# Recurrent mixer: the convolution's first tap moved from VectorE to ScalarE, the other three taps one unit later

## The reference, cut to what matters

```python
def causal_depthwise_conv(x, w, b):
    k_width = w.shape[0]
    s = x.shape[1]
    xp = jnp.pad(x, ((0, 0), (k_width - 1, 0), (0, 0)))
    out = b + xp[:, 0:s] * w[0]
    for k in range(1, k_width):
        out = out + xp[:, k:k + s] * w[k]
    return out

def recurrent_mixer(x, w_in, conv_w, conv_b, gate_a_w, gate_a_b, gate_x_w, gate_x_b, lam, w_out):
    y, r = jnp.split(x @ w_in, 2, axis=-1)
    y = jax.nn.gelu(y)
    r = causal_depthwise_conv(r, conv_w, conv_b)
    h = rg_lru(r, gate_a_w, gate_a_b, gate_x_w, gate_x_b, lam)
    return (y * h) @ w_out
```

## Time and profile before

| | before |
|---|---|
| median of 3 runs | 1528.91 us |
| lowest, highest | 1522.83, 1529.1 us |
| the profiled execution | 1525.94 us |
| its span | 1524.0 us |
| TensorE, VectorE, ScalarE, GpSimd busy | 97%, 69%, 50%, 21% of the span |
| mean granted TensorE clock | 0.994 of full speed |

### The profile page before, as it was taken

How to read it: one execution, slowest core, us unless ns; L and a number is a source line. 1 busy time by engine, 2 the same in 40 slices (tenths; PEclk the granted TensorE clock), 3 DMA queues, 4 the chain that set the end, 5 groups by cost and what they waited for, 6 DMA issues and landing times.

```text
span 1524.0 us, 31453 instructions
## 1 busy us (share of the span) xinstructions
PE 1480.7 (97%) x11939; PEld 1460.6 (96%) x11939; DVE 1052.0 (69%) x1999; ACT 765.5 (50%) x1270; POOL 318.6 (21%) x392
## 2 busy tenths in 40 slices
PE   7999998999999999999999999999999999999998
PEld 7999998899999999999999999889999999899898
DVE  6666578766655666557766656888678778876883
ACT  5454448555444554445554545446644453565442
POOL 4111113211101111014321114453320125231000
PEclk9999999999999999999999999999999999999999
DMA  6656754465555655554565555533343554334333
GB/s 207 186 179 200 241 166 139 152 189 184 181 174 185 186 184 181 173 188 154 162 192 180 179 176 157 152 107 116 91 119 107 164 145 123 99 98 125 111 117 120
DMA packets 245275, 239.65 MB, mean 157 GB/s; under 512 B 15160, under 2 KB 244392, under 8 KB 245048
## 3 DMA queue, kind: packets, MB, share of 16 engines
q1 hardware_dynamic: 245176, 238.29, 50.9%
HBM read 237.21 MB, written 1.05 MB: 156 GB/s over the span
## 4 chain that ended last, share of the span: by engine, by line
PE 84%; DVE 10%; ACT 2%; issue 2%; POOL 1%; DMA 0%; SPq 0%; DVEq 0%; ACTq 0%; POOLq 0%
PE bank L552 25%; PE bank L554 25%; PE bank L553 25%; DVE w_lo L1523 3%; PE bank L878 1%; PE bank L818 1%; PE bank L836 1%; ACT w_hi L967 1%; PE bank L801 1%; DVE work L1563 1%; DVE work L1680 1%; PE bank L884 1%; PE bank L894 1%; PE bank L817 1%; PE bank L837 0%
## 5 line engine op out<-in xcount | busy, mean ns | idle before, releaser
L1523 DVE TENSOR_TENSOR w_lo<-raw,w_hi 128x1024 fp32r<-128x1024 f32 (+1 forms) x456 | 563.0, 1244 | 303.8 <-ACT w_hi L967 303.5
L552 PE MATMUL bank<-x_hi,w_hi 128*128 128x256 f32 (+1 forms) x2480 | 719.0, 290 | 2.2 <-DVE w_lo L1523 2.2
L554 PE MATMUL bank<-x_hi,w_lo 128*128 128x256 f32 (+1 forms) x2480 | 707.1, 285 | 0.0
L553 PE MATMUL bank<-x_lo,w_hi 128*128 128x256 f32 (+1 forms) x2480 | 706.2, 285 | 0.0
L967 ACT CAST w_hi<-raw 128x1024 fp32r<-128x1024 f32 (+1 forms) x456 | 464.9, 1030 | 261.2 <-PE bank L554 250.1
L552 PEld LDWEIGHTS bank<-x_hi,w_hi 128*128 128x128 f32 x2480 | 476.0, 192 | 4.1 <-issue 2.0
L553 PEld LDWEIGHTS bank<-x_lo,w_hi 128*128 128x128 f32 x2480 | 476.1, 192 | 1.0
L554 PEld LDWEIGHTS bank<-x_hi,w_lo 128*128 128x128 f32 x2480 | 475.6, 192 | 0.0
L552 PE MATMUL bank<-y_hi,w_hi 128*128 128x256 f32 (+1 forms) x1088 | 310.2, 285 | 8.0 <-DVE y_lo L1534 8.0
L554 PE MATMUL bank<-y_hi,w_lo 128*128 128x256 f32 (+1 forms) x1088 | 309.5, 284 | 0.0
L553 PE MATMUL bank<-y_lo,w_hi 128*128 128x256 f32 (+1 forms) x1088 | 309.4, 284 | 0.0
(11 more groups left out here) (288 smaller groups left out, 1248.8 us busy)
## 6 DMA issues: line engine op xcount, KB each, us to landing
raw<-in_ffn_w_in_dram SPq DMA_DIRECT2D x176, 512.0 KB, 3.6
raw<-in_w_in_dram SPq DMA_DIRECT2D x100, 512.0 KB, 3.6
raw<-in_ffn_w_out_dram SPq DMA_DIRECT2D x64, 512.0 KB, 4.2
raw<-in_w_out_dram SPq DMA_DIRECT2D x32, 512.0 KB, 3.5
raw<-in_ffn_w_out_dram SPq DMA_DIRECT2D x32, 384.0 KB, 3.0
raw<-in_rec_w_in_dram SPq DMA_DIRECT2D x16, 512.0 KB, 3.7
raw<-in_sg_w_in_dram SPq DMA_DIRECT2D x16, 512.0 KB, 3.4
raw<-in_rec_w_out_dram SPq DMA_DIRECT2D x8, 512.0 KB, 3.4
```

The source lines that it names most:

```text
L552: mm(acc, wh, xh, start=first and j == 0, stop=False)
L553: mm(acc, wh, xl, start=False, stop=False)
L554: i_ = mm(acc, wl, xh, start=False, stop=last and j == n - 1)
L1523: TT(w_lo[:, s, 0:n, :], raw[:, s, 0:n, :], w_hi[:, s, 0:n, :].bitcast(fp32), SUB).then_inc(lo_made, 1)
```

## The change

ScalarE computes tap 0 and the bias as an Identity activation with the tap's weight as scale (`taps0`), at the end of its visits 1, 3, 5 and 7, behind the wait for `tile_read`. VectorE leaves tap 0 out and adds taps 1 to 3 one visit later: behind the `w_lo` of visits 2, 4 and 6, and for the last pair ahead of the `w_lo` of visit 8. A new semaphore `conv_tap0` ties the two. TensorE's and GpSimd's orders stay as they were.

```diff
+            def taps0(p):
+
+                for c in (2 * p, 2 * p + 1):
+                    act.wait_ge(tile_read, 2 * pb + c + 1)
+                    activation(rec_x[:, c, :], rec_p[:, c, 0:SEQ], ACT.Identity, scale=pcol("rec_conv_w", c),
+                               bias=pcol("rec_conv_b", c)).then_inc(conv_tap0, 1)
+
...
                     split_w(U + LEAD)
                     if r == 1:
                         root(1, META)
+                    if r in (1, 3, 5, 7):
+                        taps0(r // 2)
                     if r == 5:
                         gates(range(4))
...
             def conv1(p):
 
-                for k in range(4):
+                for k in range(1, 4):
                     for c in (2 * p, 2 * p + 1):
                         src, w = rec_p[:, c, k:k + SEQ], pcol("rec_conv_w", k * NC8 + c)
-                        if k == 0:
-                            i_ = TS(rec_x[:, c, :], src, w, pcol("rec_conv_b", c), MUL, ADD)
-                        else:
-                            i_ = STT(out=rec_x[:, c, :], in0=src, scalar=w, in1=rec_x[:, c, :], op0=MUL, op1=ADD)
+                        if k == 1:
+                            dve.wait_ge(conv_tap0, c + 1)
+                        i_ = STT(out=rec_x[:, c, :], in0=src, scalar=w, in1=rec_x[:, c, :], op0=MUL, op1=ADD)
...
+                    if r == 8:
+                        conv1(3)
                     if r == 9:
                         mult_squares(range(4))
...
                     split_w(U + LEAD)
                     if r == 1:
                         inverse(1, META)
+                    if r in (2, 4, 6):
+                        conv1(r // 2 - 1)
...
-                        if p < 4:
-                            dve.wait_ge(tile_read, 2 * (pb + p) + 2)
-                            conv1(p)
```

More of the change, by code:

```diff
@@ L339, in build_stack @@
             sem(n) for n in ("conv_new", "gates_mm", "gates_sig", "gated_in", "ax_new", "a2_new", "mult2", "mult_new"))
-        rec_gelu, rec_bx, scanned = sem("rec_gelu"), sem("rec_bx"), sem("scanned")
+        rec_gelu, rec_bx, scanned, conv_tap0 = sem("rec_gelu"), sem("rec_bx"), sem("scanned"), sem("conv_tap0")
         sg_gelu, sg_sqs, sg_sum, sg_rms = sem("sg_gelu"), sem("sg_sqs"), sem("sg_sum"), sem("sg_rms")
```

## The result

The changed kernel took 1535.28 us, median of 6 runs (1533.43 to 1537.8), against 1526.27 us of the kernel before, now also over 6 runs (1522.83 to 1529.1). The ratio of the runs is 1.0061, 95% interval 1.0047 to 1.0074: slower, by 9.0 us between the medians. The profiled execution of the change took 1537.8 us with a span of 1536.0 us, 12.0 more than the span before.

The account below looks back on a forecast made before the run. The stage's end was taken as bound by one chain: `decays`, the cast at 252.71 us, VectorE's queue, `y_lo`. That cast coming 8.45 us later, added to the median of 1528.91 us, gave 1537 us, range 1531 to 1541.

Parts of the forecast that it names:

- the sum of 8.45 us: Delay of ScalarE's cast at 252.71 us to 261.16, passed on through VectorE's queue and `y_lo` to the output product.
- VectorE's idle time behind the scalings: VectorE waits for ScalarE's cast before the `w_lo` behind each scaling: some 1.7 us, near 6 us at the third.
- cast of visit 8: On ScalarE behind the fourth taps and first `decays`: starts at 249.36 us, before at 238.81.
- cast ahead of the `y_lo` chain: ScalarE's cast behind the second `decays`: starts at 261.16 us instead of 252.71, 8.45 us later.
- TensorE's wait at pair 0, pair 2: Before the gate products: 2.7 us at pair 0, before 0.62; a new wait of 4.0 us at pair 2.
- The price of the tap: One Identity activation on ScalarE with 256 columns: 0.60 us, a pair 1.00 us.
- The removed taps: Eight tap-0 instructions off VectorE, 4.1 us, of which nothing is left on the path because VectorE waits longer.
- The difference of the two engines' prices: By the skill's rule, eight instructions dearer on ScalarE than VectorE would lose 0.9 us; not used in the sum.
- The clock rival: TensorE's clock falls at pair 0's gate products, adding 1.4 us to the chain: 9.8 us, 1539 us; chance 0.17.
- TensorE's slack at pair 2: TensorE waits 4.0 us at pair 2's gate products, so a clock fall there costs nothing.
- The absorbed case: ScalarE's 13.0 us idle time takes the taps in, only TensorE's first-round wait remains: 2.1 us, 1531 us; chance 0.09.
- The relieved case: VectorE is relieved and TensorE's waits for the convolution go: 2.2 to 4.1 us faster, 1525 to 1527; chance 0.04.

Follow-up runs that it names:

- e4: The change with taps of pairs 0 to 2 behind the next visit's cast on ScalarE and pair 3's behind the decays; ratio 1.0003 to the kernel before.
- e8: The changed kernel once more, unaltered, for a second trace; median 1535.25 us, ratio 1.0061 to the kernel before.
- e6: The kernel before plus eight Identity activations on ScalarE at the taps' places, needing no wait, results unread; ratio 1.0005 to the kernel before.
- e7: The change with only pairs 0 and 1's tap 0 on ScalarE, behind the next visit's cast; pairs 2 and 3 whole on VectorE; ratio 1.0004 to before.
- e5: The change plus one more Identity activation per pair between the two taps, result unread; median 1534.91 us, ratio 1.0066 to the kernel before.

## Why the prediction was right

Forecast 1537 us in 1531 to 1541, slower with 0.64; measured 1535.28 us. The forecast was added to a median of three runs, 1528.91 us; over six it is 1526.27, and 8.45 us on that is 1534.7. So 1537 was 1.7 us too high because of its base, not because of the sum. The change is slower by 0.61%, over the 0.5% that the prediction asked for, though the interval begins at 0.47%. The mechanism is what was right: the sum of 8.45 us is 8.50 in the trace. Point by point:

| step | forecast | first trace |
|---|---|---|
| scalings of pairs 1, 2, 3 start | 224.21, 231.64, 243.28 | 224.09, 231.52, 243.27 |
| VectorE's idle time behind the scalings | 1.7, 1.7, near 6 | 1.76, 1.77, 6.10 |
| cast of visit 8 | 249.36 | 249.34 |
| cast ahead of the `y_lo` chain | 261.16 | 261.11 |
| output product | 277 | 276.96 |
| TensorE's wait at pair 0, pair 2 | 2.7, 4.0 | 2.71, 3.88 |

- **The price of the tap** was taken from the same instruction of the later mixer, 0.60 us, and measured 593 ns in the median:

```profile
L1062 ACT ACTIVATE work<-work,par x8: 584/593/603, 217.1 to 244.2; 128x256 f32<-128x256 f32 x8
```

- **The removed taps** gained nothing on the path, as forecast: VectorE is busy 1046.0 us instead of 1052.0, but stands idle before its `w_lo` 21.8 us in this stretch, where it was 6.6.
- **The difference of the two engines' prices**, 0.9 us, which the sum left aside, isn't what was lost: with all eight taps on ScalarE, e4 is 0.34 us longer than before, the change 8.50.
- **The clock rival.** It was put as a dearer outcome, 9.8 us, if TensorE's clock fell at pair 0. In the first trace it didn't fall there (1.00 from 222 to 230 us), in e8 it did (0.61 from 222 to 224, 0.53 from 224 to 226), and the distance was the same. What was wrong in this rival is its price of 1.4 us. ScalarE's cast of visit 5 and the `w_lo` behind it, VectorE's and ScalarE's timelines of e8:

```profile
229.32 1.05 ACT L967 CAST w_hi<-raw 128x1024 fp32r<-128x1024 f32 x1 [2.56 <-PE bank L554]
```

```profile
230.57 1.22 DVE L1532 TENSOR_TENSOR w_lo<-raw,w_hi 128x1024 fp32r<-128x1024 f32 x1
```

The cast came 1.6 us later than in the first trace (227.73), of which 0.2 are a later start of the whole stage, not 3 us, and ended at 230.37, before VectorE asked. The low clock lasted shorter than the six microseconds that I had read from a later stage: the mean from 222 to 230 us is 0.79.
- **TensorE's slack at pair 2** held: there the clock did fall (0.63 from 242 to 246 us) and nothing on ScalarE waited for it. In e8 TensorE came to pair 2 later, by the fall at pair 0, and waited 2.48 us there instead of 3.88.
- **The absorbed case** is close to what e6 shows, but for work without the wait. **The relieved case** has next to no support: with all taps out of the way (e4) the distance isn't shorter, and the best order tried (e7) is 0.42 us shorter, not 2.2.
- What the sum left out is the scatter: a change of 8.5 us in place gave 9.0 and 10.6 in two sets of medians, 12.0 between the first two spans.

## What to carry to other kernels

Before moving work to an engine with idle time, look at what its queue holds behind the new instruction and whom the new instruction waits for. If it waits for engine A and A's next instruction needs something that stands behind it in the same queue, the two engines run in turn, and idle time is no measure of room. The cure tried here was not less work but order: the feeding instruction first, the new one behind it, which took 8.2 of the 8.5 us back. Compare traces by a distance between two landmarks around the change (equal to 0.01 us between two executions here) where totals scatter by more than the effect.

## What was not expected of the hardware

TensorE's granted clock after the same wait at the same place differs between executions of one kernel. In both traces TensorE was busy with matmuls throughout from 216 to 220 us at 1.00 and then waited 2.71 us at pair 0; behind that the clock was 1.00 in the first trace and, in the windows of e8, this:

```profile
222.00:224.00 2.00, 1.02 (x3) 0.87 (x4) 1.97 (x4) 0.00 (x0) 0.00 (x0) 0.61 0.68 240
224.00:226.00 2.00, 2.00 (x7) 1.61 (x6) 1.03 (x3) 1.26 (x3) 0.00 (x0) 0.53 0.23 72
```

So a fall can't be forecast from the wait alone. And one more activation per round cost the chain 0.49 us each time (e5), less than the 0.59 us that one takes, since neighbours on ScalarE overlap: from the first of two taps to the next instruction it is 1.00 us here (217.14 to 218.14), 1.03 in the later mixer.
